# A later copy of the condition's rows, and the second attention's squares added up by VectorE alone

## The reference

```python
# first block: the condition scales and shifts the normed input
mod   = silu(c) @ w_mod + b_mod           # the same for c_ctx
sh1, sc1, g1, sh2, sc2, g2 = split(mod, 6)
h     = rms_norm(x, norm1_w) * (1 + sc1) + sh1
hc    = rms_norm(ctx, norm1_w) * (1 + sc1c) + sh1c
p     = h @ w_in                          # queries, keys, values, gates

# second block: attention_mixer
xn    = x * rsqrt(mean(x * x, axis=-1) + eps) * g
proj  = xn @ w_in                         # q, k, v and the forget gates
...
h     = h + conv_ffn(...)                 # and so on, to the last down-projection
```

## Time and profile before

| | us |
|---|---|
| median of 3 runs | 1234.12 |
| lowest, highest | 1234.0, 1234.75 |
| the profiled execution's own time | 1233.9 |
| its span, first to last instruction | 1232.1 |
| TensorE matmuls busy in it | 1220.7 (99%) |
| VectorE, GpSimd, ScalarE busy | 748.1, 714.4, 668.9 |

### The profile page before, as it was taken

How to read it: one execution, slowest core, us unless ns; L and a number is a source line. 1 busy time by engine, 2 the same in 40 slices (tenths; PEclk the granted TensorE clock), 3 DMA queues, 4 the chain that set the end, 5 groups by cost and what they waited for, 6 DMA issues and landing times.

```text
span 1232.1 us, 24305 instructions
## 1 busy us (share of the span) xinstructions
PE 1220.7 (99%) x8626; PEld 1096.8 (89%) x8626; DVE 748.1 (61%) x1639; ACT 668.9 (54%) x1205; POOL 714.4 (58%) x308
## 2 busy tenths in 40 slices
PE   8999999999999999999999999999999999999998
PEld 5788889877799999999988779999999999899998
DVE  5796667455641766665626664766667325766665
ACT  6333334454544755555755537666666546666663
POOL 5476553442168765557595306665575986755573
PEclk9999999999999999999999999999999999999999
DMA  9968542231135554556474304554563754555461
GB/s 345 373 253 313 189 160 82 85 104 53 52 109 183 155 205 172 186 185 214 126 221 122 101 2 121 187 203 167 191 221 121 221 175 142 188 198 191 169 220 51
DMA packets 58188, 208.11 MB, mean 169 GB/s; under 512 B 6640, under 2 KB 7808, under 8 KB 58112
## 3 DMA queue, kind: packets, MB, share of 16 engines
q1 hardware_dynamic: 57888, 206.56, 49.3%
q0 software_dynamic: 224, 0.52, 0.1%
HBM read 206.01 MB, written 1.05 MB: 168 GB/s over the span
## 4 chain that ended last, share of the span: by engine, by line
PE 94%; DVE 3%; ACT 1%; issue 1%; DMA 1%; POOL 0%; SPq 0%; DVEq 0%; ACTq 0%
PE ps L547 19%; PE ps L548 18%; PE ps L549 18%; PE ps L573 13%; PE ps L575 6%; PE ps L591 2%; PE ps L815 2%; PE ps L593 2%; PE ps L594 2%; PE ps L886 1%; PE ps L912 1%; PE ps L901 1%; DMA X<-in_xc 1%; PE ps L860 1%; PE ps L1031 1%
## 5 line engine op out<-in xcount | busy, mean ns | idle before, releaser
L333 POOL TENSOR_TENSOR wlo<-raw,whi 128x1024 fp32r<-128x1024 f32 x287 | 697.8, 2445 | 489.8 <-ACT whi L1277 443.1
L1277 ACT ACTIVATE whi<-raw 128x1024 fp32r<-128x1024 f32 x338 | 353.1, 1054 | 117.7 <-PE ps L549 53.7
L547 PE MATMUL ps<-H,whi 128*128 128x256 f32 (+3 forms) x1312 | 386.9, 295 | 1.4 <-DVE H L1814 1.1
L548 PE MATMUL ps<-H,whi 128*128 128x256 f32 (+3 forms) x1312 | 376.9, 287 | 0.0
L549 PE MATMUL ps<-H,wlo 128*128 128x256 f32 (+3 forms) x1312 | 376.8, 287 | 0.0
L547 PEld LDWEIGHTS ps<-H,whi 128*128 128x128 f32 (+1 forms) x1312 | 249.8, 190 | 15.0 <-issue 9.3
L548 PEld LDWEIGHTS ps<-H,whi 128*128 128x128 f32 (+1 forms) x1312 | 250.3, 191 | 2.5
L549 PEld LDWEIGHTS ps<-H,wlo 128*128 128x128 f32 (+1 forms) x1312 | 249.6, 190 | 2.5
L573 PE MATMUL ps<-H,whi 128*128 128x512 f32 x672 | 238.9, 398 | 0.0
L2211 DVE SCALAR_TENSOR_TENSOR arena<-ps,sm,arena 128x256 f32<-128x256 f32 (+2 forms) x264 | 127.5, 483 | 102.4 <-ACT arena L1535 95.2
L575 PE MATMUL ps<-H,wlo 128*128 128x256 f32 x672 | 188.7, 281 | 0.0
(11 more groups left out here) (338 smaller groups left out, 1521.6 us busy)
## 6 DMA issues: line engine op xcount, KB each, us to landing
raw<-in_stream SPq DMA_DIRECT2D x386, 512.0 KB, 4.2
X<-in_xc SPq DMA_DIRECT2D x4, 512.0 KB, 5.9
out_y<-X SPq DMA_DIRECT2D x8, 128.0 KB, 2.0
kx<-in_const SPq DMA_DIRECT2D x1, 512.0 KB, 8.4
params<-in_params SPq DMA_DIRECT2D x1, 344.0 KB, 5.9
kx<-in_const POOLq DMA_DIRECT2D x1, 256.0 KB, 4.5
k<-in_const POOLq DMA_DIRECT2D x1, 129.0 KB, 5.5
k<-in_const SPq DMA_DIRECT2D x1, 128.0 KB, 5.5
```

The source lines that it names most:

```text
L333: pool.tensor_tensor(wlo[:, slot, :], raw[:, rslot, :], whi[:, slot, :].bitcast(f32), ALU.subtract).then_inc(rest_done[0], 1)
L547: pe.matmul(out, lh, rh, start=start, stop=False, skip_group_check=True)
L548: pe.matmul(out, lh, rl, start=False, stop=False, skip_group_check=True)
L1277: act.activation(whi[:, s % RING, :], raw[:, r % RING, :], ACT.Copy).then_inc(hi_done, 1)
```

## The change

Two edits, independent of each other.

At the start, ScalarE no longer copies the spread condition into `c_across` before the first chunk's high parts; the copy and its wait stand behind them.

At the second attention, VectorE adds the four sums of pairs further: sum 0 and 1, sum 2 and 3, then those two, three more additions of 128x256. TensorE takes one matmul instead of four, behind value block 2 instead of block 1. GpSimd's wait before the rest of block `S_ATT2 + 2` asks for all seven additions instead of four. The other waits on `sq_sum` only count three more.

```diff
@@ gpsimd
                     if s == S_ATT2 + 2:
-                        pool.wait_ge(S["sq_sum"], 4 * 3)
+                        pool.wait_ge(S["sq_sum"], 4 * 2 + KC - 1)
                     if s in LATE_STARTS:
-                        pool.wait_ge(S["sq_sum"], 4 * LATE_STARTS[s] + 4)
+                        pool.wait_ge(S["sq_sum"], 4 * LATE_STARTS[s] + 4 + (3 if LATE_STARTS[s] > 2 else 0))
@@ tensor: sumsq
-                pe.wait_ge(S["sq_sum"], 4 * n + i + 1)
+                pe.wait_ge(S["sq_sum"], 4 * n + i + 1 + (3 if n > 2 else 0))
@@ tensor: value blocks of the second attention
-                if k == 1:
-                    for i in range(KC // 2):
-                        sumsq(2, i)
+                if k == 2:
+                    pe.wait_ge(S["sq_sum"], 4 * 2 + KC - 1)
+                    pe.matmul(ss_out(2), ones, sq[:, 0, 0:T], start=True, stop=True).then_inc(S["ss_ready"], 1)
@@ scalar: start
             splits_upto(0)
-            act.wait_ge(S["c_bc"], 1)
-            act.activation(c_across, PS[:, 2:4, :].rearrange("p b n -> p (b n)"), ACT.Copy)\
-               .then_inc(S["c_across"], 1)
             for k in range(KC):
...
+                if k == 0:
+                    act.wait_ge(S["c_bc"], 1)
+                    act.activation(c_across, PS[:, 2:4, :].rearrange("p b n -> p (b n)"), ACT.Copy)\
+                       .then_inc(S["c_across"], 1)
                 if k in SPLITS_BEHIND:
                     splits_upto(SPLITS_BEHIND[k])
@@ vector: behind the last chunk of the second attention's norm
                     if k % 2 == 0:
                         sum_pair(2, k - 1)
+            for n, (to, by) in enumerate(((0, 2), (4, 6), (0, 4))):
+                dve.wait_ge(S["sq_sum"], 4 * 2 + (6 if n == 2 else 4))
+                dve.tensor_tensor(sq[:, to, 0:T], sq[:, to, 0:T], sq[:, by, 0:T], ALU.add)\
+                   .then_inc(S["sq_sum"], 1)
```

## The result

| | before | after |
|---|---|---|
| median, us | 1234.45 (10 runs, 1233.93 to 1240.33) | 1238.12 (10 runs, 1237.57 to 1242.54) |
| ratio after to before | | 1.0033, 95% interval 1.0021 to 1.0044 |
| profiled execution, us | 1233.9 (span 1232.1) | 1238.75 (span 1236.9) |

The changed kernel is slower by 0.33%, 3.7 us of the medians. The forecast was 1237.2 with a range of 1235.0 to 1238.5, and slower as the likeliest sign.

What follows compares the result with a forecast made beforehand. TensorE, busy 99% of the span, was taken to bound the kernel. 1233.9 - 0.1 (start) + 1.7 (lateness and sum) + 1.5 (clock) = 1237.0, plus 0.2 to the median: 1237.2, range 1235.0 to 1238.5.

Steps and rivals of the forecast that it cites:

- Start, gain of 0.8 locally: At the start, with the copy behind the high parts, TensorE's first product starts at about 20.35 instead of 21.15.
- 0.1 in the end: Of the start's gain only 0.1 us lasts, as TensorE then waits for `w_mod` transfers; bounds 0 and 0.8.
- The leads of 0.2 and 0.13 us: How far ahead of need the `w_mod` transfers at about 33.85 and 46.12 arrive in the kernel before.
- Lateness of GpSimd, 1.25 us: Second attention: GpSimd starts block 2's rest behind three more additions, at 608.65 instead of 607.40, so TensorE's block 2 is late.
- Lateness, one sum and the restart, 1.7 together: Second attention: block 3 starts 1.25 + 0.43 + 0.05 later, 1.7 us; bounds 1.25 and 1.85.
- The clock: TensorE's 3.06 us pause before block 2 drops its clock to half for 3 us, costing 1.5 us; bounds 1.0 to 2.1.
- the clock that stays up: Rival: the pause before block 2 does not lower TensorE's clock, small gain at the start, time 1235.7; chance 0.24.
- The gain at the start lasts whole: Rival: the start's 0.8 us is kept to the end; 1236.5 with the clock falling, 1235.0 without; chance 0.10.
- the additions hide: Rival: the second attention's three additions cost nothing, the edit wins 1.89 - 0.43, time about 1232.7; chance 0.04.
- Block 7: Second attention: the later reciprocal root delays block 7's high part and rest, but TensorE does not wait; covered by 2.4 us.
- the base: Starting time of the sum: profiled execution of the kernel before, 1233.9 us, plus 0.2 to the median of the runs.

Runs made afterwards that it cites:

- the copy alone: The kernel before with only the start's edit, the moved copy of the condition's rows: 1235.98 us, ratio 0.9998.
- the version with the wait at block 3: The changed kernel with GpSimd's wait for seven additions moved from block 2's rest to block 3's: 1236.83 us; repeated, 1233.08 us.
- the kernel that has only this: The kernel before, four sums kept, plus three additions into unread chunks and GpSimd waiting for all seven: 1237.38 us, ratio 1.002.
- the pause filled: The changed kernel with six extra matmuls of 256 columns behind block 1, their result overwritten unread: 1236.42 us, ratio 1.0009.
- the sums alone: The kernel before with only the second attention's edit, the start's copy left as before: 1238.19 us, ratio 1.0016.

## Why the prediction was right or wrong

**Start, gain of 0.8 locally: right; 0.1 in the end: not contradicted.** 20.38 against 20.35 forecast, and 0.1 us in the undisturbed runs, which is within their spread. The mechanism (the `w_mod` loads take it back) is right too, and where it takes it back depends on the execution. In the profiles of the changed kernel and of the copy alone it is a transfer at 28 to 30 us that held TensorE 1.1 us, one that I had not listed since before it had arrived in time; in the repeat of the version with the wait at block 3 it is the one near 34 us that I had named, with a wait of 0.4. The leads of 0.2 and 0.13 us that I read off one profile are themselves a matter of the execution: the four other traces without the move wait 0.3 to 1.1 us at the one near 34.

**Lateness of GpSimd, 1.25 us: right.** 1.26 in the trace, and 1.2 as a difference of time in the kernel that has only this, in its one run at 1.000; the traced stretch is 1.21 us longer there (214.33 against 213.12).

**Lateness, one sum and the restart, 1.7 together: right.** 1.73 in the traces with the pause filled. The undisturbed runs give 1.5, where it should be 1.6 with the start's 0.1 taken off.

**The clock: the price right, the place wrong.** I expected the clock to fall within the pause and bounded the pause from which a fall comes by one number, the 2.1 us behind the last matmul. The clock stayed at 1.00 through all 3.02 us of the pause and fell at about 613.5, after 0.8 us of block 2, whose first matmuls started 0.23 to 0.33 us apart and only the later ones 0.43. That is 3.8 us behind the end of block 1's last matmul, where the program's end had 2.1. So that step failed, and with it the one number as a bound. That the low level then held 3.4 us where I had put 3, and cost 1.5 where I had put 1.5, is in part luck, since I had worked it out from a fall in the middle of the pause. The 4.2 us at the beginning were a weak support too: the windows of those first 6 us show a granted clock of 1.00 while the matmuls are 0.45 us apart, so the low level there is read off the distance alone.

I gave the clock that stays up a chance of 0.24, and more in the other cases. In the runs of the sums alone 11 of 12 are under a mean of 1.000, all of them at 1237.28 or more, and even after 2.03 us the fall is there. The rival with the clock up came in one run of twelve. Its time looks right by luck (1235.7; 1235.60 was measured): over the undisturbed runs beside it that run is 0.8 us, where the rival has 1.6 and the runs with the filled pause 1.5.

**The other rivals.** "The gain at the start lasts whole" and "the additions hide" are contradicted by the rows above. Block 7 didn't wait.

**What was mis-sized is the base: the profiled execution and the 0.2 us to its median.** The forecast was 1234.12 + 3.1, where the changed place measures 1.73 + 1.51. The measured median is 1238.12, 0.9 us more. Of this, 0.1 us is the changed place, and 0.3 us is that the kernel before itself has a median of 1234.45 over ten runs; beside the experiments its undisturbed runs are at 1234.57 to 1234.84. The profile that I started from was an early one: TensorE's first `sumsq` is at 410.45 there and at 411.11 to 411.75 in the four other traces that have the same start and no chance fall. The five runs at 0.999, which fits the fall at the changed place alone, have a median of 1237.62, 3.2 over 1234.45. The other 0.5 us comes from the other half of the runs, which have a mean of 0.997 or 0.994 and take 1238.5 to 1242.5: a further fall (the profiled execution has it behind 9 us) or several. My sum went from one profiled execution and three runs that agreed within 0.8 us, and took for granted that the rest of the program would run undisturbed as there. That term was put at nothing without a reason: it is nothing in half of these ten executions and 1 to 5 us in the others. Four of the ten lie above the range's 1238.5. How many do so is chance of the ten in part: in the sums alone it was two of twelve at such a mean.

## What to carry to other kernels

When work is taken off the busiest engine, look first whether it lay in the shadow of a wait. Here the four sums did, and what replaced them stood on the very chain that the engine waited for; with the wait one block further on, where there is slack, the same edit takes 1.45 us off the traced stretch, though over all runs no gain is shown. Price a pause of TensorE twice: its length (with the sum 1.7 us here), and the work behind it at half the clock (1.5 us). And where single executions differ by more than the effect, group the runs by their mean clock and compare the groups beside the medians of all; the groups leave out what an edit may do to the share of long runs.

## What was not expected of the hardware

- TensorE's clock fell after pauses of 3.0 and of 2.03 us between dense stretches, each time not in the pause but 0.1 to 0.8 us after the matmuls had begun again (612.5 with a start at 612.35 in the sums alone; 611.4 with 610.83; 613.5 with 612.69), and came back 3.4 us later.
- It also fell where TensorE had no pause. The row before such a fall in the copy alone, and the windows around it, with PE busy throughout:

```profile
227.78 1.98 PE L860 MATMUL ps<-rows,kx 4*128 4x512 f32 x4
```

```profile
230.00:231.00 1.00, 1.00 (x11) 1.00 (x10) 0.96 (x4) 0.78 (x3) 0.00 (x0) 1.00 0.00 0
231.00:232.00 1.00, 1.00 (x8) 1.00 (x7) 0.82 (x3) 0.92 (x5) 0.00 (x0) 0.54 0.00 0
232.00:233.00 1.00, 1.00 (x6) 1.00 (x6) 0.90 (x4) 1.00 (x1) 0.00 (x0) 0.50 0.00 0
```

The fall comes at about 231.1, 1.4 us behind four matmuls that read 4 partitions instead of 128. The kernel before runs the same matmuls and kept 1.00 in its trace; whether they have a part in it, no run here shows.

- A VectorE addition of 128x256 took 2.5 us beside GpSimd's subtractions, 0.42 alone, while GpSimd's took 2.55 to 2.60 us instead of 2.35 to 2.42.
